# Spare TensorE products in the waits of a two-layer encoder kernel

## The reference

```python
for i in range(DEPTH):                     # DEPTH = 2
    h = rmsnorm(x, norm_mix[i])
    x = x + (windowed_attention if i % 2 == 0 else gated_deltanet)(h, ...)
    h = rmsnorm(x, norm_ffn[i])
    x = x + hierarchical_moe(h, ...)       # 4 groups x 8 experts
```

## Time and profile before

| | us |
|---|---|
| median of three runs | 1319.03 |
| the three runs | 1319.03, 1319.50, 1305.58 |
| the profiled execution | 1311.08 |
| its span, first to last instruction | 1309.5 |
| PE busy | 1157.9 (88%) |
| DVE / ACT / POOL busy | 541.1 / 376.2 / 364.2 |
| mean granted TensorE clock | 0.951 |
| chain that ended last: PE / DMA / DVE / ACT | 66% / 13% / 11% / 4% |

### The profile page before, as it was taken

One profiled execution on the slowest core, in us unless ns is written; L12 is line 12 of the kernel. 1 busy time (PEld: TensorE's weight loads), 2 busy tenths in 40 slices (PEclk: granted clock), 3 DMA queues, 4 the chain that ended last, 5 costly groups with the idle time before them and its releaser, 6 DMA issues.

```text
span 1309.5 us, 21136 instructions
## 1 busy us (share of the span) xinstructions
PE 1157.9 (88%) x8573; PEld 823.1 (63%) x8573; DVE 541.1 (41%) x1210; ACT 376.2 (29%) x830; POOL 364.2 (28%) x412
## 2 busy tenths in 40 slices
PE   5999999899999886689878999779999899999782
PEld 4867778755555443668667887569888555555441
DVE  4565853521111112755575455674563411111113
ACT  3424650111111011245544354553341111111110
POOL 1332000113223221045644257544301122222110
PEclk8997999989999999689989999899999799999996
DMA  7121016899999998411000111000546999999996
GB/s 235 65 71 65 2 52 263 335 351 382 379 387 381 379 390 323 177 65 65 1 2 3 65 65 65 2 3 1 225 177 261 345 359 379 391 389 370 387 395 251
DMA packets 67793, 278.21 MB, mean 212 GB/s; under 512 B 16888, under 2 KB 16984, under 8 KB 43120
## 3 DMA queue, kind: packets, MB, share of 16 engines
q1 hardware_dynamic: 56480, 255.89, 51.4%
q0 software_dynamic: 11072, 20.43, 4.6%
q10 hardware_dynamic: 144, 0.52, 0.1%
HBM read 265.83 MB, written 27.26 MB: 224 GB/s over the span
## 4 chain that ended last, share of the span: by engine, by line
PE 66%; DMA 13%; DVE 11%; ACT 4%; SPq 3%; issue 2%; POOL 1%; DVEq 0%; POOLq 0%; ACTq 0%
PE bank L1016 13%; PE bank L144 9%; PE bank L146 8%; PE bank L145 8%; PE bank L1025 6%; DMA hn<-in_moe_w_up 5%; PE bank L1558 3%; PE bank L1008 3%; DMA ring<-in_moe_w_up 3%; DMA arena<-in_moe_w_up 2%; PE bank L506 2%; DMA ring<-in_gdn_w_in 2%; PE bank L487 2%; PE bank L282 2%; PE bank L496 2%
## 5 line engine op out<-in xcount | busy, mean ns | idle before, releaser
L893 POOL DMA_INDIRECT y_rows<-arena,idx_i x64 | 64.6, 1009 | 347.9 <-DVE arena L1202 347.9
L1206 DVE TENSOR_TENSOR arena<-arena,bank 128x128 f32<-128x128 f32 x64 | 18.4, 288 | 257.5 <-ACT arena L1107 257.5
L1107 ACT ACTIVATE arena<-bank 128x128 f32<-128x128 f32 x64 | 17.7, 277 | 366.5 <-PE bank L1016 222.7
L146 PE MATMUL bank<-ring_r,ht_r 128*128 128x512 f32 x288 | 113.1, 393 | 0.0
L1016 PE MATMUL bank<-ring,arena 128*64 128x256 f32 x832 | 101.6, 395 | 8.6 <-DMA ring<-in_moe_w_up 7.6
L1202 DVE COPY arena<-bank 128x512 f32<-128x512 f32 x64 | 44.3, 692 | 144.1 <-PE bank L1025 144.1
L144 PE MATMUL bank<-ring_r,arena_r 128*128 128x512 f32 (+1 forms) x228 | 91.4, 401 | 5.1 <-DVE ring_r L168 5.1
L145 PE MATMUL bank<-ring_r,arena_r 128*128 128x512 f32 x224 | 88.1, 393 | 0.0
L1016 PEld LDWEIGHTS bank<-ring,arena 128*64 128x64 f32 x832 | 57.8, 136 | 43.6 <-DMA ring<-in_moe_w_up 8.5
L145 PE MATMUL bank<-ht_r,ring_r 128*128 128x512 f32 (+1 forms) x224 | 82.3, 368 | 0.0
L1008 PEld LDWEIGHTS bank<-ident,arena 64*128 64x128 f32 x512 | 61.3, 201 | 28.3 <-issue 25.1
(11 more groups left out here) (330 smaller groups left out, 2371.8 us busy)
## 6 DMA issues: line engine op xcount, KB each, us to landing
ring<-in_moe_w_gate SPq DMA_DIRECT2D x26, 1024.0 KB
ring<-in_moe_w_up SPq DMA_DIRECT2D x26, 1024.0 KB
arena<-in_moe_w_down SPq DMA_DIRECT2D x24, 1024.0 KB
ring<-in_moe_w_down SPq DMA_DIRECT2D x24, 1024.0 KB
ring<-in_gdn_w_in SPq DMA_DIRECT2D x8, 2048.0 KB, 8.2
arena<-in_moe_w_gate SPq DMA_DIRECT2D x10, 1024.0 KB
arena<-in_moe_w_up SPq DMA_DIRECT2D x10, 1024.0 KB
ht<-in_moe_w_gate SPq DMA_DIRECT2D x10, 1024.0 KB
```

What stands on the lines that cost most here:

```text
L146: return pe.matmul(dst, a[1], b[0], start=False, stop=stop)
L893: pool.indirect_dma_start(out=y_rows[l], out_offset=bass.IndirectOffsetOnAxis(ap=idx_i[:, 1, e:e + 1], axis=0), in_=y_out[:, e % RING, :], ...
```

## The change

A function `spare_pe(pe, n, b)` issues `n` spare products into bank `b`. They are placed so:

- in `project_back_pe`, one between the last transposes and the last router product, behind a wait for the last addition into `x`;
- in `moe_pe`, three, a wait for the first signal of `s["dve"]` (the group is found), and four, in place of the six; four behind the rank products; two at the head of `pick_rows`;
- in `inverse_pe` of `p` 0 and 2, two behind each of the two `first_m`, each behind a wait for `g["a"]`, and three between the two `by_side` products of `l == 1`, into bank 2;
- between the layers, a wait for the first `combined` and six, then two behind the transposes of tile 0 and three behind those of tile 1.

```diff
--- before.py
+++ after.py
@@ -342,6 +342,8 @@
             route_pe(pe, k, tpk + 1, TT - 2)
             pe.wait_ge(ln["rows"], TT * (2 * k + 1) + TT)
             turn_routed(pe, k, tpk + 1, TT - 1)
+            pe.wait_ge(x_half, 2 * TT * (k + 1))
+            spare_pe(pe, 1, 3)
             route_pe(pe, k, tpk + 1, TT - 1)
 
         def turn_routed(pe, l, k, t):
@@ -977,13 +979,19 @@
                 eng.wait_ge(late_dma[l], LATE * LATE_DMA)
                 eng.wait_ge(late_weights[l], LATE * LATE_WEIGHTS)
 
+        def spare_pe(pe, n, b):
+
+            for _ in range(n):
+                pe.matmul(bank[b][:, 0:KC * (GROUPS + EXPERTS)], ones[:, :], router[:, 0].rearrange("p c n -> p (c n)"),
+                          start=True, stop=True)
+
         def pick_bank(half):
             return bank[5 + 2 * half]
 
         def moe_pe(pe, l):
-            for _ in range(6):
-                pe.matmul(bank[3][:, 0:KC * (GROUPS + EXPERTS)], ones[:, :], router[:, l].rearrange("p c n -> p (c n)"),
-                          start=True, stop=True)
+            spare_pe(pe, 3, 3)
+            pe.wait_ge(s["dve"], 1 + l * PER["dve"])
+            spare_pe(pe, 4, 3)
             pe.wait_ge(s["onehots"], 1 + l * PER["onehots"])
 
             pe.matmul(bank[1][:, 0:TT * EXPERTS], upper[:, :], oh_sum.rearrange("p t e -> p (t e)"),
@@ -1029,6 +1038,7 @@
                 return last
 
             def pick_rows():
+                spare_pe(pe, 2, 3)
                 pe.wait_ge(pick["made"], PICK["made"] + 1 + l)
                 for t in range(TT):
                     for half in range(2):
@@ -1645,8 +1655,12 @@
                 pe.wait_ge(g["exps"], 4 * p + 4)
                 for slot in range(2):
                     first_m(pe, 2 * p + slot, 3 * slot + 1)
+                    pe.wait_ge(g["a"], 2 * p + 1)
+                    spare_pe(pe, 2, 2)
             for l in range(1, LEVELS):
                 for slot in range(2):
+                    if first and l == 1 and slot:
+                        spare_pe(pe, 3, 2)
                     if 1 < l < TOP:
                         pe.wait_ge(g["sn"], at_level(p, l - 1, slot))
                         if l == 2 and not first:
@@ -2432,9 +2446,12 @@
                 turn_pe(pe, 1, t)
             project_back_pe(pe, 0, 3, 1)
             moe_pe(pe, 0)
+            pe.wait_ge(s["combined"], 1)
+            spare_pe(pe, 6, 3)
             for t in range(2):
                 pe.wait_ge(ln["rows"], 2 * TT + t + 1)
                 turn_pe(pe, 3, t)
+                spare_pe(pe, 2 + t, 3)
             for t in range(2):
                 turned(pe, 3, t)
             for U in range(2):
```

## The result

The changed kernel ran in 1305.43 us (median of 20 runs, 1297.2 to 1309.42), the kernel before beside it in 1313.07 us (20 runs, 1305.58 to 1319.5). The medians differ by 7.6 us, the means (1304.04 and 1313.25) by 9.2. The ratio, which goes by the means, is 0.9931 with a 95% interval of 0.9912 to 0.995: 9.1 us less, between 6.6 and 11.6. The forecast was 11.1 us from a level of 1313.8, so 1303. The profiled execution took 1297.91 us, its span 1296.3 us, and the mean granted clock was 0.970; before it was 1311.08 us, 1309.5 us and 0.951. The other 9.1 are as much as the timed difference.

The account below looks back on a forecast made before the run. TensorE, busy for 88% of the span, was taken as the bound, with the weights' DMA deep in the mixtures. From 1313.8 us, 1.7 + 3.3 + 2.5 + 3.6 = 11.1 us less gave 1302.7, said as 1303; range 1291 to 1316.

Parts of the forecast that it names:

- The price of a spare: Everywhere: one spare product costs TensorE 0.5 us at the full clock and 0.93 us at the lower.
- First routing: Layer 0's routing: `pick_rows` falls from 9.41 to 7.2 us, starting 0.2 late; gain 2.0 us, 1.7 in the sum.
- Second routing: Layer 1's routing: router product 0.95, `pick_rows` 2.7, gate and up 1.55 us less; at best 4.8, 3.3 in the sum.
- Between the layers: Gap after layer 0: first two halves at full clock take 5.8 us instead of 8.54; 2.5 us in the sum.
- Inverse heads: Head of both inverse stages: 64-column products and `rows_pe` at full clock, 2.0 us each; 3.6 us in the sum.
- The weights hide the routings: Rival, mixtures of experts: the DMA stream catches up nothing, the routings' 5 us are lost, 1308 us; chance 0.10.
- All the lower clock comes back: Rival, seven low-clock windows: all time lost to the clock, 24 us, returns, 1290 us; chance 0.12, mostly for 14 to 18.
- The clock falls anyway: Rival, gaps between spares and short products: light work lets the clock fall; gain 0 to 3 us, 1312; chance 0.08.
- Slower, spares in front of real work: Rival, all places: spares running at the lower clock delay real products by 14.6 us in all, 1328 us; chance 0.08.

Follow-up runs that it names:

- the narrow one: The change with its added spare products 8 columns wide instead of 288, the six at each routing's head as before: 1310.96 us, ratio 0.9989 to the kernel before.
- the first expert's spares: The change plus one spare ahead of and one behind the transposes of the first expert's rows: 1299.02 us, ratio 0.9905 to the kernel before.
- the kernel with the most spares: The change plus one spare each side of the first expert's transposes, four in the attention, seven in layer 1's projections: 1297.78 us, ratio 0.9884 to the kernel before.

## Why the prediction was right, step by step

- **The price of a spare, 0.5 or 0.93 us.** Right at both levels: at full clock four took 2.02 us to the next start (0.51 each) and seven 3.98 from first start to last end (0.57 each); six between the layers took 5.55 to the next start (0.93).
- **First routing, 1.7 (at best 2.0).** Measured 1.83. `pick_rows` at 7.03 to 7.13 us was forecast as 7.2, and its start did not move. One step behind it failed without harm to the sum: the clock was to stay up, and gate and up went from 3.84 to 5.32 us. I had thought of the spares up to `pick_rows` and not of the two waits of 0.78 us with eight short transposes between them that follow. Between the two profiled executions the routing therefore gained only 2.3 - 1.5 = 0.8 us (30.49 to 29.69). The mean gain is 1.83 because the kernel before was in a good state there: without spares, the four other profiles take 31.4 to 32.2 us, three with the last router product at the lower clock (3.32 us instead of 1.95 in the kernel with spares between the layers alone), the narrow one with its lists (3.67 instead of 1.89). In the changed kernel and its repeat neither is so slow (1.94 and 2.11 us, the lists 1.89). So this term was right by luck, by two errors that cancel: the gate and up that was overlooked (1.5 us), and a base that I read from one execution (1.1 us).
- **Second routing, 3.3 (at best 4.8).** Measured 3.70. Made up otherwise than said: `pick_rows` 2.8 instead of 2.7, its start 1.0 earlier as forecast, and of the 1.55 us for gate and up nothing. The kernel with two spares around the first transposes shows that these 1.5 us were to be had in its stage, in both layers, but in layer 1 only some 0.7 of them last to the end of the mixture.
- **Between the layers, 2.5.** Measured 2.27. The first products start 25.73 us after the last down product instead of 25.43, 0.3 us late where up to 0.6 was allowed, and two halves took 5.8 us, as forecast.
- **Inverse heads, 3.6.** Measured 3.83 at the heads, and 2.1 after what is given back later. This is the step that was wrong: "Together 2.0 us ... so they are on the path" looked at the head only. What the clock does in the second pair changed too, by 0.85 us a stage in the mean; in the two profiles of the change itself by nothing in the first half and 1.3 us in the second. The timed runs put the part between none and some 10 us and don't settle it further.
- **The weights hide the routings (0.10).** Fallen: the rest of a mixture has the same length with and without, so what the change wins before it comes through, and the DMA share in the last window rose from 0.76 to 0.97. It returns for the next 1.6 us: with the first expert's spares the share is 1.01 there, and 0.9 of them are lost in layer 1.
- **All the lower clock comes back (0.12).** Fallen: it priced the lower clock at 24 us, and 9 came. Of the mean clock's 0.049 below full only 0.019 came back. The Trainium skill, "TensorE: Matmul & The Clock Gate", section "HAM oscillation", halves the throttled time for the penalty; here that sum is 24 us and the measured gain about two fifths of it. Part of the throttled time was spares and waits, as the prediction argued; and the change did not bring the whole clock back. Its Part 1 puts the ramp at less than 1% of a typical kernel's span; the 0.69% measured lies under it, and the 1.16% of the kernel with the most spares (0.76 to 1.57) above, so no run here confirms that bound.
- **The clock falls anyway (0.08).** True in three places (the first gate and up, the second pair of the inverse, and at times the spares behind the ranks), not as the whole result.
- **Slower, spares in front of real work (0.08).** Not in the change's own two profiles. Doubled, the same code shows it at full clock, 11.1 us by the stages. At the lower clock it shows in 4 of the 16 routings with these spares, each with `pick_rows` 1.5 us late.

## What to carry to other kernels

Where TensorE waits for short steps of another engine, look at the granted clock of the dense work that comes next: here 288-column products in those waits cut 0.7% from a tuned kernel, while 8-column ones at the same places did nothing. Fill the wait and no more; twice as many gave all of it back. The price at the lower clock (0.93 us here, against 0.5) is the careful measure of what fits, though no run here compares the two measures. Judge such edits by the lengths of stages over several profiles, and look also for falls of the clock behind the stage, for half of a part that shows 2 us in its own stage may be given back there.

## What the runs showed that I had not expected

- The clock does not need one long wait to fall. Behind stretches in which TensorE was busy for a good part with short products it fell all the same: 2.25 of 5 us busy at 675 in the kernel without head spares, with waits of 1.31 and 1.43 us, then 0.52.
- The same code falls in one profile and not in another. The first half fell in neither profile of the change, and in all three kernels that add spares only elsewhere and keep those of its head (by 2.6, 1.3 and 2.6 us). The second half fell in all five.
- The scatter of a run has a place. The attention alone spans 8.3 us between the profiles, and its length goes with the clock granted in it: 244.0 us at 1.00, 252.4 at 0.95, whatever was changed behind it.
- 90 runs of the unchanged kernel had mean clocks of 0.941 to 0.959 and took 1306.1 to 1324.4 us, correlated at -0.92, 9.6 us for each 0.01 of clock. The 20 runs of the change have a mean of 0.967, those 90 one of 0.952; by that slope the 0.015 would be some 15 us, and it brought 9. The slope is not the worth of clock won by spares, which is in part spent on the spares themselves.
- Two kernels at the same mean clock over their runs differ by 14.7 us: 0.972 for the one with the first expert's spares (1299.02 us) and for the doubled one (1313.7 us). The mean clock is no measure of such a change.
